# Late gate products as half units in the first half's delta rule, joined outputs of two chunks, and no products in the inverse's first level

## The reference, cut to what matters

```
kb, vb = k * beta, v * beta                        # chunks of 64 tokens
a_mat = where(strict, kb @ k^T * decay, 0);  t_mat = a_mat + I
u, w = triangular_solve(t_mat, [vb, kb * exp(gcum)])
for each chunk:
    v_new = u - w @ S
    o     = (q * exp(gcum)) @ S + (q @ k^T * decay) @ v_new
    S     = S * exp(g_last) + (k * exp(g_last - gcum))^T @ v_new
```

## Time and profile before

| | us |
|---|---|
| median of three runs | 4057.0 |
| profiled execution | 4054.38 |
| its span | 4052.6 |
| TensorE busy in it | 3413.6 (84%) |
| DVE busy | 2170.6 (54%) |
| ACT busy | 975.3 (24%) |
| granted TensorE clock, mean of the span | 0.91 |

### The profile page before, as it was taken

One profiled execution on the slowest core, in us unless ns is written; L12 is line 12 of the kernel. 1 busy time (PEld: TensorE's weight loads), 2 busy tenths in 40 slices (PEclk: granted clock), 3 DMA queues, 4 the chain that ended last, 5 costly groups with the idle time before them and its releaser, 6 DMA issues.

```text
span 4052.6 us, 46601 instructions
## 1 busy us (share of the span) xinstructions
PE 3413.6 (84%) x17225; PEld 2225.7 (55%) x17225; DVE 2170.6 (54%) x4791; ACT 975.3 (24%) x2214; POOL 1370.4 (34%) x1537
## 2 busy tenths in 40 slices
PE   7788999999999989899979999988788977544444
PEld 3455544555555578788868888765455633111111
DVE  3567036452232278311353246787666567788875
ACT  3665114300000032210341221115423312112111
POOL 0000000264222200000000026655545677777775
PEclk9898999999999999999988999999888988676667
DMA  5325920543434224654311349999768999999998
GB/s 195 125 96 179 323 77 17 183 174 119 153 111 161 116 89 157 214 194 147 129 61 63 125 159 390 412 406 346 276 210 316 401 394 410 409 409 409 401 402 341
DMA packets 340349, 942.24 MB, mean 233 GB/s; under 512 B 25800, under 2 KB 104085, under 8 KB 327989
## 3 DMA queue, kind: packets, MB, share of 16 engines
q0 software_dynamic: 150832, 565.17, 36.3%
q1 hardware_dynamic: 188896, 373.81, 25.6%
q10 hardware_dynamic: 420, 0.62, 0.0%
HBM read 911.21 MB, written 102.76 MB: 250 GB/s over the span
## 4 chain that ended last, share of the span: by engine, by line
PE 61%; DVE 15%; DMA 7%; ACT 6%; issue 6%; POOL 5%; SPq 0%; DVEq 0%; POOLq 0%; ACTq 0%
PE bank L885 22%; PE bank L2995 8%; DMA arena<-in_peer_v,arena 4%; PE bank L2964 4%; PE bank L3212 3%; PE bank L2736 3%; DVE ring L2570 3%; POOL ring L1379 3%; POOL arena L1394 2%; PE bank L2799 1%; PE bank L2927 1%; PE bank L2951 1%; PE bank L3077 1%; DMA ring<-in_peer_u,arena 1%; PE bank L2641 1%
## 5 line engine op out<-in xcount | busy, mean ns | idle before, releaser
L3212 PE MATMUL bank<-arena 64*64 64x512 f32 x2720 | 413.8, 732 | 263.2 <-DMA arena<-in_peer_v,arena 251.1
L1379 POOL DMA_INDIRECT ring<-in_peer_u,arena x512 | 539.8, 1054 | 282.2 <-issue 137.9
L1394 POOL DMA_INDIRECT arena<-in_peer_v,arena x424 | 448.3, 1057 | 279.1 <-PE bank L3212 120.3
L885 PE MATMUL bank<-hT,ring 128*128 128x256 f32 (+1 forms) x1536 | 445.2, 452 | 2.5 <-ACT hT L786 2.3
L885 PE MATMUL bank<-arena,ring 128*128 128x256 f32 (+1 forms) x1536 | 442.1, 450 | 0.0
L2570 DVE SCALAR_TENSOR_TENSOR ring<-ring,bank 128x1024 f32<-128x1024 f32 x256 | 311.7, 1220 | 150.5 <-DMA ring<-in_peer_u,arena 143.0
L2995 PE MATMUL bank<-hT,ring 128*128 128x256 f32 x1536 | 363.9, 396 | 25.5 <-DVE hT L2283 25.4
L3212 PEld LDWEIGHTS bank<-arena 64*64 64x64 f32 x2720 | 103.7, 156 | 508.4 <-DMA arena<-in_peer_v,arena 340.1
L885 PEld LDWEIGHTS bank<-hT,ring 128*128 128x128 f32 x1536 | 292.7, 191 | 153.7 <-issue 120.4
L885 PEld LDWEIGHTS bank<-arena,ring 128*128 128x128 f32 x1536 | 292.3, 190 | 148.4 <-issue 121.3
L2995 PEld LDWEIGHTS bank<-hT,ring 128*128 128x128 f32 x1536 | 300.7, 199 | 92.8 <-issue 38.1
(11 more groups left out here) (564 smaller groups left out, 5513.6 us busy)
## 6 DMA issues: line engine op xcount, KB each, us to landing
ring<-in_mlp_w SPq DMA_DIRECT2D x32, 2048.0 KB, 9.0
ring<-in_ada_w SPq DMA_DIRECT2D x24, 2048.0 KB, 9.6
late_weights<-in_mlp_w SPq DMA_DIRECT2D x32, 1024.0 KB, 12.7
ring<-late_weights SPq DMA_DIRECT2D x32, 1024.0 KB, 8.3
ring<-weights_kept SPq DMA_DIRECT2D x32, 1024.0 KB, 8.5
s_store<-arena POOLq DMA_DIRECT2D x8, 2816.0 KB, 9.7
ring<-in_w_in SPq DMA_DIRECT2D x10, 2048.0 KB, 8.0
arena<-s_store SPq DMA_DIRECT2D x16, 1024.0 KB, 6.1
```

The lines of the kernel that those rows point to most:

```text
L885: last = pe.matmul(bank[:, 0:hi - lo], w[:, k, m * P:(m + 1) * P], x[:, k, lo:hi], start=(k == 0), stop=(k == 7))
L1379: pool.indirect_dma_start(u_row[k % ERING], None, I["peer_u_2"][0], bass.IndirectOffsetOnAxis(idxs[:, k // EXPERTS, k % EXPERTS:k % EXPERT ...
L1394: pool.indirect_dma_start(v_row[v_slot(v)], None, I["peer_v_2"][0], bass.IndirectOffsetOnAxis(idxs[:, v // EXPERTS, v % EXPERTS:v % EXPERT ...
L3212: last = pe.matmul(banks[2 * r + n][QUADS[r if y == 0 else 1 - r], :], diag[QUADS[r], (v + y) % V_SLOTS, :], v_row[v_slot(v + y)][QUADS[r] ...
```

## The change

Late gate products: `glu` n becomes `gla` n and `glb` n on TensorE, eight matmuls each, both in one bank (columns 0 to 255 and 256 to 511). Products 4 and 7 take a bank from the turn, the others bank 2. ACT marks its sigmoid by a semaphore of its own, and DVE's drain alone frees the bank. The places on each engine are given by the new `GATE_AT`. Seven of the halves now stand ahead of the inverse's end, four between `sa` and `sc` of each chunk.

The `z` projections of the first half move forward: 0 and 1 after `qkv` 9, 2 after `qkv` 11, 3 between `pb` 0 and `pa` 1. The inverse's first level multiplies by the identity once (a transpose) and subtracts from it; `eye` sets nothing and `ib` 0 is gone. `so` 0 to 3 become `sv` 0 and 1, one for two chunks, with four state buffers in three places. These two hold for both halves. SP loads gate block 0 ahead of `kv_read`.

```diff
 # side_order
-    yield from steps("qkv", 8, 10) + steps("gs", 0, 4) + steps("gr", 0, 4) + steps("qkv", 10, 11) + ...
+    yield from steps("qkv", 8, 10) + steps("z", 0, 2) * first + steps("gs", 0, 4) + steps("gr", 0, 4) + ...
+    yield from steps("gq", 4, 8) + steps("qkv", 11, 12) + steps("z", 2, 3) * first + steps("gs", 4, 8) + ...
+    yield from steps("vtok", 0, 2) + steps("ktok", 0, 2) + [("pa", 0), ("pb", 0)] + steps("z", 3, 4) * first + [("pa", 1), ("pb", 1)]
     for lv in range(6):
         yield "ia", lv
-        yield "ib", lv
+        if lv:
+            yield "ib", lv
...
         yield "sc", n
-        yield "so", n
+        if n % 2:
+            yield "sv", n // 2
-GATE_AT = {("ib", 0): (0,), ("ib", 1): (1,), ("ib", 2): (2,), ("ib", 3): (3,), ("ib", 4): (4,), ("uw", 1): (5,), ("os", 3): (6, 7)}
+GATE_AT = {
+    "PE": {("gr", 7): (("gla", 0), ("glb", 0)), ("vtok", 1): (("gla", 1),), ("ktok", 1): (("glb", 1),), ("pb", 1): (("gla", 2),), ("ib", 2): (("glb", 2),),
+           ("ib", 4): (("gla", 3),), ("uw", 1): (("glb", 3),), ("sa", 0): (("gla", 4),), ("sa", 1): (("glb", 4),), ("sa", 2): (("gla", 5),),
+           ("sa", 3): (("glb", 5),), ("sv", 1): (("gla", 6),), ("os", 3): (("glb", 6), ("gla", 7), ("glb", 7))},
+    "ACT": {("gn", 7): (("glu", 0),), ("ktok", 1): (("glu", 1),), ("ib", 2): (("glu", 2),), ("uw", 1): (("glu", 3),), ("sa", 1): (("glu", 4),),
+            ("sa", 3): (("glu", 5),), ("on", 3): (("glu", 6), ("glu", 7)), ("gq", 3): (("z", 0), ("z", 1)), ("pb", 1): (("z", 3),)},
+    "DVE": {("gn", 7): (("glu", 0),), ("pa", 0): (("glu", 1),), ("ia", 3): (("glu", 2),), ("sa", 0): (("glu", 3),), ("sc", 1): (("glu", 4),),
+            ("sc", 3): (("glu", 5),), ("on", 3): (("glu", 6), ("glu", 7))}}
+GATE_ROTATES = (4, 7)
 # side_tickets
+        if step == "gla" and n not in GATE_ROTATES:
+            t.append((f"glu{h}_{n}", 1, (2,)))
+        elif step == "gla":
+            t.append((f"glu{h}_{n}", 1, (banks[turn % len(banks)],)))
 # DVE, level 0
+                    if n == 0:
+                        for y in range(2):
+                            dve.wait_ge(S("g_level"), 12 * h + y + 1)
+                            dve.tensor_tensor(inv_xt[:, y], bc4(ident[:, :]), g_lvl[:, y], ALU.subtract).then_inc(S("g_inverse"), 1)
+                            bank = filled(dve, t + y)
+                            drained(dve.tensor_tensor(inv_x[:, y], bc4(ident[:, :]), heads(bank[:, :]), ALU.subtract), t + y)
 # TensorE
-                if step == "glu":
+                if step in ("gla", "glb"):
...
+                    bank = claim(pe, t) if half == 0 else ps[bank_of[t]]
+                    for k in range(KD):
+                        last = pe.matmul(bank[:, half * HALF:(half + 1) * HALF], w[:, k, c:c + P], late_y[:, k, :], ...)
+                elif step == "sv":
+                    bank = claim(pe, t)
+                    for hd in range(4):
+                        y = bank[:, hd * P:(hd + 1) * P]
+                        pe.matmul(y, v_new[:, hd * P:(hd + 1) * P], attnT[:, n, hd, :], start=True, stop=False)
+                        for c in range(2):
+                            cols = slice(c * GCH, (c + 1) * GCH)
+                            last = pe.matmul(y[:, cols], g_state[2 * n + c][:, hd, :], qkvT[:, hd, n * P + c * GCH:n * P + (c + 1) * GCH], start=False, stop=(c == 1))
```

More of the change, by code:

```diff
@@ L261, in side_order @@
     yield from [("qkv", 3), ("ls", 2), ("ls", 3)] + steps("qkv", 4, 8) + steps("gq", 0, 4)
[L262 to L267, removed]
+    yield from steps("qkv", 8, 10) + steps("z", 0, 2) * first + steps("gs", 0, 4) + steps("gr", 0, 4) + steps("qkv", 10, 11) + steps("gn", 0, 4)
+    yield from steps("gq", 4, 8) + steps("qkv", 11, 12) + steps("z", 2, 3) * first + steps("gs", 4, 8) + steps("gr", 4, 8)
+    yield from steps("z", 0, 1) * (not first) + steps("gn", 4, 8) + steps("z", 1, 4) * (not first)
+    yield from steps("vtok", 0, 2) + steps("ktok", 0, 2) + [("pa", 0), ("pb", 0)] + steps("z", 3, 4) * first + [("pa", 1), ("pb", 1)]
     yield "eye", 0
@@ L283, in side_order @@
     yield from steps("wo", 0, 8) + steps("fsq", 0, 8) + steps("fsum", 0, 1) + steps("fscl", 0, 8) + steps("pq", 0, 16)
-GATE_AT = {("ib", 0): (0,), ("ib", 1): (1,), ("ib", 2): (2,), ("ib", 3): (3,), ("ib", 4): (4,), ("uw", 1): (5,), ("os", 3): (6, 7)}
-GATE_TAKEN = {"PE": {}, "ACT": {("os", 3): ("on", 3)}, "DVE": {**{("ib", n): ("ia", n + 1) for n in range(5)}, ("uw", 1): ("sa", 0), ("os", 3): ("on", 3)}}
+GATE_AT = {
[7 more added lines that the diff above has]
+GATE_ROTATES = (4, 7)
 def first_order(engine):
-    gates = {GATE_TAKEN[engine].get(at_, at_): ns for at_, ns in GATE_AT.items()}
+    moved = {s for ss in GATE_AT[engine].values() for s in ss if s[0] == "z"}
     for step, n in side_order(0):
-        yield 0, step, n
-        for m in gates.get((step, n), ()):
-            yield 1, "glu", m
+        if (step, n) not in moved:
+            yield 0, step, n
+        for s, m in GATE_AT[engine].get((step, n), ()):
+            yield (0 if s == "z" else 1), s, m
         if (step, n) == ("fscl", 7):
@@ L1232, in _ @@
             sp.dma_start(kv_read, kv_kept).then_inc(S("kv_moved"), 16)
-            sp.wait_ge(S("weights_kept"), 16 * (len(TAIL_WEIGHTS) + 8 + len(LATE_BLOCKS)))
-            for j in range(4):
+            for j in range(1, 4):
                 load_block(sp, block0["glu1"] + j, gate_weights[j])
@@ L2939, in side @@
                 o, x, t = HALVES[h], HT * h + n, ticket0.get(f"{step}{h}_{n}")
-                if t is None:
+                if t is None and step not in ("gla", "glb"):
                     return
                 tok = slice(n * P, (n + 1) * P)
-                if step == "glu":
+                if step in ("gla", "glb"):
+                    t, half = ticket0[f"glu{h}_{n}"], "ab".index(step[2])
+                    w, c = block(pe, block0["glu1"] + n // 2, KD), 256 * half + n % 2 * P
                     if n == 0:
                         pe.wait_ge(S("x_landed1"), 64)
-                    w = block(pe, block0["glu1"] + n // 2, KD)
-                    for half in range(2):
-                        c = 256 * half + n % 2 * P
-                        bank = claim(pe, t + half)
-                        for k in range(KD):
-                            last = pe.matmul(bank[:, 0:HALF], w[:, k, c:c + P], late_y[:, k, :], start=(k == 0), stop=(k == KD - 1))
-                        fill(last, t + half)
+                    bank = claim(pe, t) if half == 0 else ps[bank_of[t]]
+                    for k in range(KD):
+                        last = pe.matmul(bank[:, half * HALF:(half + 1) * HALF], w[:, k, c:c + P], late_y[:, k, :], start=(k == 0), stop=(k == KD - 1))
+                    if half == 1:
+                        fill(last, t)
                 elif step == "lsum":
@@ L3100, in side @@
                     for hd in range(4):
-                        last = pe.matmul(bank[r, hd * P:(hd + 1) * P], wT[h][:, hd, n * GCH:(n + 1) * GCH], g_state[N % 2][:, hd, :], start=True, stop=True)
+                        last = pe.matmul(bank[r, hd * P:(hd + 1) * P], wT[h][:, hd, n * GCH:(n + 1) * GCH], g_state[n][:, hd, :], start=True, stop=True)
                     fill(last, t)
```

70 lines of the change are left out of this document (35 added, 35 removed).

## The result

The kernel after takes 4019.5 us (median of 4 runs, 4008.6 to 4021.9) against 4057.1 (4052.9 to 4058.6) for the kernel before on the same chip: ratio 0.9897, 95% interval 0.9885 to 0.9909. The profiled execution took 4008.6 us, span 4006.7; it is the fastest of the four, the other three took 4018 to 4022. So the traces put before and after 45.9 us apart and the medians 37.6. A control run of the same kernel, with five rounds, gave 4018.1 and the ratio 0.9890 (0.9877 to 0.9902).

A forecast was written before the change was run, and what follows sets the result against it. Serial work ahead of the DMA-bound gather was taken as the bound, with TensorE lacking slack in the inverse. Terms 3 - 30.3 - 0.5 - 5.3 - 7 = -40.1 took 4054.4 to 4014.3, stated as 4016 us; range 4003 to 4035.

The forecast's parts named there:

- the stretch from `ia` 0 to `sa` 0: Sign in the first half's inverse: this stretch lasts 50 to 53 us if the forecast is right.
- `w2` starts 33.4 us earlier: Sign at the end of the first half: `w2` was to start some 33 us earlier.
- the granted clock of the recurrence: Sign in the first half's recurrence: granted clock above 0.85, where it had been 0.55.
- Term 1: Up to the inverse: waits for bank 2 and gate block 1, with cold starts, cost +3 us (-2 to +8).
- Term 2: First half's inverse: gate products leave, first level shrinks, some waits lose cover; -30.3 us (-33 to -26).
- Term 3: Recurrence up to first `os`: halves added at full clock, 3 us allowed for low-clock spells; -0.5 us (-6 to +25).
- Term 4: `os` to `w2`: less TensorE work, normalisation then late by under 1 us; -5.3 us (-6 to -2).
- Term 5: Second half in the gather: shorter first level and joined outputs, part given back; -7 us (-13 to +3).
- (a): Rival: first half gains as said, second half nothing because rows then wait for transfers; 4023 us, chance 0.20.
- (b): Rival: the clock stays low in the first half's recurrence; 4044 us, chance 0.08.
- (c): Rival: clock lost in the wait for bank 2 stays at 1.2 GHz up to `w2`; 4110 us, chance 0.04.
- (d): Rival: each product in bank 2 waits for the one before, five reuses costing 8 us each; near 4046, chance 0.05.

The follow-up runs named there:

- bank_in_turn: Changed kernel with gate product 1 in a bank of the turn instead of bank 2; 4014.0 us, ratio 0.9898 to the kernel before.
- gates_only: Kernel before plus gate halves, early `z` and new bank rule, with old first level and separate `so` in both halves; 4044.0 us, ratio 0.9957.
- halves_grouped: Changed kernel with the recurrence's four gate halves moved in front of `sa` 0; ratio 0.9935 to the kernel before.
- z_first_ticks: Changed kernel with `z` 3 ahead of `ktok` and second-half ticks from the old sum of costs; 4011.1 us, ratio 0.9890 to before.
- second_half_only: Kernel before with only the second half's new first level, joined outputs and new ticks; 4047.2 us, ratio 0.9966.

## Why the prediction was right

The terms of the prediction add up to -40.1 us; the two medians are 37.6 us apart, those of the control's batch 42.6. Of its signs, the stretch from `ia` 0 to `sa` 0 took 53.4 us in the first trace, just outside the 50 to 53, and 51.8 in the control; `w2` starts 33.4 us earlier, counted from m, and the granted clock of the recurrence is 1.00.

**Term 1, up to `ia` 0: forecast +3, measured +2.5** (+3.4 and -0.9; the control has +3.4 and +0.9). Both waits are where they were put. That to `pa` 0 was 1.4 short. The drain came where forecast, 117 us behind m; the wait is 5.95 instead of 5.2 only because `vtok` 1, counted from m, ended 1.0 us earlier than before the change. What was short is the cold start: `gla` 1 ran in 6.21 instead of 3.45 plus the 1 us allowed. The cold start I had read off as 1.7 us for 16 records of 128 columns; for the wider gate product it is 2.6. Block 1 came as forecast, 2.59 us late, but `gla` 2 ran warm in this execution and cold, 5.41, in the control and in `bank_in_turn`.

**Term 2, the inverse: forecast -30.3, measured -28.1 (control -29.7).** Sizes and signs of each part hold: the two waits are 2.08 us each (forecast 2.1), that behind level 0 1.69 us (forecast 2.0 with its subtractions). The 1.6 us between the two executions are one cold spell, `ia` at 2119.31 with 3.66 instead of 2.05 us, as the windows of 4 us of the changed kernel show (columns as in the last fence):

```profile
2116.00:2120.00 4.00, 1.92 (x16) 0.94 0.00 0
2120.00:2124.00 4.00, 4.00 (x25) 0.64 0.00 0
```

I had taken a clock of 0.98 in an inverse with short open waits as a sign that 2.1 us cost nothing more. They do in some executions.

**Term 3, the recurrence: forecast -0.5, measured -3.0.** The working at full clock, 34.0 us, was right (34.6); wrong were the 3 us allowed for spells at the low clock. There are none: the clock is 1.00 in all seven traces that have the halves within the recurrence and `sv`. What I had not seen is that it needs both: the halves alone leave 0.88 and 43.0 us (`gates_only`), `sv` alone 0.65 and 34.3 us with four halves less (`halves_grouped`). I gave the clock's rise to the halves, and the joined outputs to a count of calls. Joined outputs with no gate halves do stay at 1.00 in the second half's recurrence, in all nine traces that have them; there the gather's products stand between the steps. `sv` took 2.82 us (2174.07 to 2176.89), forecast 2.9.

The Trainium skill (TensorEngine Tiling (Array Packing), Key Properties) has it that a change of tiling mode drains the array. It points the right way: a call of 64 columns stands at 0.20 us in `sv`, where the rows of the array stay 128 (0.40 from 2174.39 for two), and at 0.36 in `so`, where they alternate. Its lower end, 0.11 a call, wasn't reached.

**Term 4: forecast -5.3, measured -4.8.** `w2` waits 0.73 us for the last DVE instruction of the normalisation, and starts 15.1 us after `os` (forecast 14.7). The earlier trace rows have `w2` at 2248.41, so the stretch before was 19.9 us, not the 20.0 of the prediction.

The sum up to `w2` is -33.4 against the -33.1 of the terms. That is partly luck: terms 1 and 3 came out 0.5 and 2.5 better than forecast, terms 2 and 4 2.2 and 0.5 worse.

**Term 5, the second half: forecast -7, measured -6.6 by the traces.** The mean from `w2` to the end is 1807.1 us over the five traces with the old second half and 1800.5 over the eight with the new one (without `z_first_ticks`), -6.6. Between the first two traces alone it was -8.7. The five go from 1798.5 to 1814.3, so the -6.6 is uncertain by some 3 us, and the timed runs of `second_half_only` give more, 0.34% or 13.8 us (9 to 19). The size holds by the traces, the parts don't, and that they meet is luck. By the same means the inverse gives 6.0 us instead of 4.4 (93.7 to 87.8). The recurrence gives 8.3 (34.5 to 26.2) instead of 3.3: 5.2 where the clock had held and more where it had not, a case that the one profile I had doesn't show. And 5.0 us go back in w2>2pa (645.1 to 650.1), 1.6 in 2pa>2ia and 1.1 behind `os`, in the rhythm of the gather. So 14.3 us were gained and 7.7 given back, where the prediction had 7.7 and 0.7.

**The rivals.** (a), nothing in the second half, falls by `second_half_only` (0.34%, 0.22 to 0.46). (b), the low clock, did not come, but it was nearer than 0.08 says: a part of it comes as soon as either of two parts is missing. (c) falls: after 5.95 us of wait `gla` 1 was cold and the step behind it warm, 1.04 us for `ktok`. (d) falls: no later half in bank 2 waits for DVE.

The Trainium skill (TensorE: Matmul & The Clock Gate, HAM oscillation) says that waits between bursts throttle the clock again. The trace agrees for the cold starts behind 5.95, 2.38 and 2.08 us of wait, and not for `gla` 2 of the kernel after, which ran warm behind 2.59. The falls in the recurrence of `gates_only`, 4.9 us together, had no wait ahead of them: TensorE is busy all of the 43 us.

## What to carry to other kernels

Look at the granted clock of a serial stretch before counting its instructions: work moved into thin, chained products can cost next to nothing if it lifts their clock (34.6 us with four gate halves, 34.3 without), and the same work in front of them costs its full price (13.8 us here, with the thin stretch as long as ever). Such a gain may need two edits at once, so test each with the other absent. Fill a wait with a step that also frees what the next step needs: `z` 3 moved ahead by four places took away both the wait for a drain and the one for a transfer.

## What the hardware showed unexpectedly

- The clock can fall without an idle moment: 43.0 us busy of 43.0, clock 0.88, `sa` from 1.09 to 1.97 us. What preceded were eight products of 64 columns that alternate 128 and 64 rows. The same eight were followed by a warm `sa` at two other places of that trace, so they alone don't decide it.
- The same program has it one time and not the next: the second half's recurrence at 1.00 and 31.4 us, or at 0.79 and 38.0. Part of the spread of the kernel before (4049.3 to 4065.8 us in one batch) may come from this; that it does is not shown, since only a few of the executions have a trace.
- A wait of 2.08 us was followed by `ia` in 2.05 us at 2137.51 and by one in 3.66 at 2119.31, in one execution. What decides between them the runs leave open.
- Two 64-column calls in a row take 0.40 us, two that alternate the rows of the array 0.73 (2174.40 to 2175.13 in `gates_only`, 0.36 and 0.37).
